# Hybrid decoder trunk on one core: key norms summed by a matrix of ones, five score products instead of six, rotary half turns by SBUF transfers

## The reference, cut to what matters

```python
q = (rms_norm(c_q, cq_g) @ w_uq).reshape(b_, t_, MLA_HEADS, QK_HEAD)      # 8 heads, 128 + 64 wide
ckv = rms_norm(c_kv, ckv_g)
k_nope = (ckv @ w_uk).reshape(...);  v = (ckv @ w_uv).reshape(...)
k = jnp.concatenate([k_nope, k_r], axis=-1)          # k_r: the 64 rotary key rows, the same for all heads
q = rms_norm(q, qn_g);  k = rms_norm(k, kn_g)        # over the 192 channels of a head
q, k = (rotary embedding on the last 64 channels)    # [x1 c - x2 s, x2 c + x1 s]
o = causal_block_attention(q, k, v)
```

## Time and profile before

| | |
|---|---|
| runs of the kernel | 1753.0, 1754.93, 1754.62 us; median 1754.62 us |
| profiled execution, its own time | 1751.97 us |
| its span | 1750.2 us |
| PE busy | 1734.3 us, 99% of the span, 12264 matmuls |
| DVE, ACT, POOL busy | 813.8, 467.3 and 1183.7 us |
| matmuls of `product`, share of the chain that ended last | 83% |
| one pair of heads (third pair of layer 0, from 348.8 to 446.3 us) | 97.5 us, of which PE is busy 97.4 |

### The profile page before, as it was taken

One profiled execution on the slowest core, in us unless ns is written; L12 is line 12 of the kernel. 1 busy time (PEld: TensorE's weight loads), 2 busy tenths in 40 slices (PEclk: granted clock), 3 DMA queues, 4 the chain that ended last, 5 costly groups with the idle time before them and its releaser, 6 DMA issues.

```text
span 1750.2 us, 32871 instructions
## 1 busy us (share of the span) xinstructions
PE 1734.3 (99%) x12264; PEld 1626.1 (93%) x12264; DVE 813.8 (46%) x1373; ACT 467.3 (27%) x843; POOL 1183.7 (68%) x1365
## 2 busy tenths in 40 slices
PE   7999999999999999999999999999999999999999
PEld 7999999999999999999999999989998888888887
DVE  7755546455555452212347546464555554422221
ACT  4423223242323331101134232332323233311110
POOL 7754746374798777777766647473847988777773
PEclk9999999999999999999999999999999999999999
DMA  4321212122322223222431312222222222422233
GB/s 158 123 96 54 90 59 84 65 74 70 109 84 84 84 96 130 88 96 85 161 112 64 105 56 74 72 84 68 72 77 104 85 93 86 145 88 92 96 121 110
DMA packets 47489, 161.60 MB, mean 92 GB/s; under 512 B 5408, under 2 KB 6816, under 8 KB 47136
## 3 DMA queue, kind: packets, MB, share of 16 engines
q1 hardware_dynamic: 41328, 146.56, 24.6%
q10 hardware_dynamic: 6112, 14.39, 2.2%
HBM read 152.27 MB, written 10.81 MB: 93 GB/s over the span
## 4 chain that ended last, share of the span: by engine, by line
PE 96%; DVE 2%; ACT 1%; issue 0%; ACTq 0%; DVEq 0%
PE slots L508 83%; PE slots L566 4%; PE slots L599 3%; PE slots L542 2%; PE slots L660 2%; PE slots L584 1%; PE slots L551 1%; DVE h_lo L1099 1%; DVE branch_lo L1111 1%; DVE h_tile L1175 0%; PE slots L701 0%; DVE spare L1120 0%; PE slots L569 0%; ACT cq_hi L849 0%; DVE early L1165 0%
## 5 line engine op out<-in xcount | busy, mean ns | idle before, releaser
L420 POOL TENSOR_TENSOR w_lo<-w_raw,w_hi 128x256 fp32r<-128x256 f32 x1004 | 828.4, 855 | 20.9
L415 POOL TENSOR_SCALAR w_hi<-w_raw 128x1024 fp32r<-128x1024 f32 x251 | 284.0, 1131 | 388.1 <-PE slots L508 380.7
L508 PE MATMUL slots<-h_hi,w_hi 128*128 128x264 f32 (+1 forms) x2112 | 522.8, 311 | 0.6
L508 PE MATMUL slots<-h_lo,w_hi 128*128 128x264 f32 (+1 forms) x2112 | 515.9, 308 | 0.0
L508 PE MATMUL slots<-h_hi,w_lo 128*128 128x264 f32 (+1 forms) x2112 | 515.1, 308 | 0.0
L508 PEld LDWEIGHTS slots<-h_hi,w_hi 128*128 128x128 f32 x2112 | 342.7, 188 | 22.9 <-issue 3.9
L508 PEld LDWEIGHTS slots<-h_hi,w_lo 128*128 128x128 f32 x2112 | 342.0, 188 | 19.1
L508 PEld LDWEIGHTS slots<-h_lo,w_hi 128*128 128x128 f32 x2112 | 342.0, 188 | 17.6
L508 PE MATMUL slots<-branch_hi,w_hi 128*128 128x264 f32 (+1 forms) x576 | 144.0, 313 | 9.6 <-DVE branch_lo L1111 8.9
L508 PE MATMUL slots<-branch_lo,w_hi 128*128 128x264 f32 (+1 forms) x576 | 142.8, 311 | 0.0
L508 PE MATMUL slots<-branch_hi,w_lo 128*128 128x264 f32 (+1 forms) x576 | 142.4, 311 | 0.0
(11 more groups left out here) (243 smaller groups left out, 2825.0 us busy)
## 6 DMA issues: line engine op xcount, KB each, us to landing
w_raw<-w_units SPq DMA_DIRECT2D x251, 512.0 KB, 3.2
stream<-sc_acc ACTq DMA_DIRECT2D x16, 264.0 KB, 3.0
sc_back<-stream SPq DMA_DIRECT2D x2, 2112.0 KB, 8.7
x_old<-stream SPq DMA_DIRECT2D x16, 264.0 KB, 4.4
stream<-residual_or_merged ACTq DMA_DIRECT2D x16, 264.0 KB, 2.5
ab_raw<-w_units SPq DMA_DIRECT2D x8, 512.0 KB, 4.6
residual_or_merged<-xt ACTq DMA_DIRECT2D x4, 528.0 KB, 7.6
stream<-xt ACTq DMA_DIRECT2D x1, 2112.0 KB, 10.3
```

Source lines behind the costliest of these rows:

```text
L415: pool.tensor_scalar(hi, raw, 1.0, 1.0, ALU.mult, ALU.mult).then_inc(sem("hi_part"), 1)
L420: op = pool.tensor_tensor(lo[:, cols], raw[:, cols], hi[:, cols].bitcast(F32), ALU.subtract)
L508: mm = pe.matmul(out[:, a_, 0:t1 - t0], w(k), x(k)[:, t0:t1], start=(n == 0), stop=(n == 3 * ks - 1))
```

## The change

1. The key norms no longer go by token sums and a diagonal. `spread_sum` multiplies a full matrix of ones with the squares themselves (two float32 products of 264 columns per head), so that each token's sum stands at once on all 128 partitions. It is issued right after `vb`. DVE adds the rotary part (`kr_sum`, made once per layer), ACT takes the root of the 128x528 tile, and DVE the reciprocal of the 128x528 tile, for each head. The ten sums `stat_k`, `spread_k0` and `spread_k1` and the ten diagonal pieces are gone.
2. The half turn is no product any more. ACT issues four transfers from SBUF to SBUF, of 32 rows each, as soon as DVE has written the rotary queries; the minus sign is in the sine table. The same once per layer for the rotary keys.
3. The rotary keys of a head are kept in both halves of the partitions (`kr_hi`, 128 rows), and `qr_both` holds for each head the high part of its rotary queries in 64 rows and the low part in the other 64. One product with `kr_hi` then gives hi x hi and lo x hi together: five products per score chunk instead of six.
4. The order in CQ is rearranged (`kr` before `q1`; the DVE work on `q1` later), and FILLS begins 5, 9 instead of 2, 12, with the sum of fills before the scores unchanged.

The core of the diff:

```diff
-FILLS = (2, 12, 5, 5, 6, 6, 7, 2, 6, 6, 7, 7, 6)
+FILLS = (5, 9, 5, 5, 6, 6, 7, 2, 6, 6, 7, 7, 6)
...
+            def spread_sum(out, squares):
+                for a_ in range(2):
+                    mm = pe.matmul(out[:, a_, 0:HALF], ones[0:squares.shape[0], :],
+                                   squares[:, a_ * HALF:(a_ + 1) * HALF], start=True, stop=True)
+                return mm
...
-                             (qn_lo[:, h, :], kn_hi[:, h, :]), (qr_hi, kr_hi[:, h, :]),
-                             (qr_hi, kr_lo[:, h, :]), (qr_lo, kr_hi[:, h, :])]
+                             (qn_lo[:, h, :], kn_hi[:, h, :]), (qr_both[:, h, :], kr_hi[:, h, :]),
+                             (qr_both[:, h, :], kr_lo[:, h, :])]
...
-                latent("kr", 4)
+                latent("q1", 4)
...
-                token_sums(out, [kr_sq[0:ROPE]]).then_inc(sem("cq_mm"), 1)
+                spread_sum(out, kr_sq[0:ROPE]).then_inc(sem("cq_mm"), 1)
...
+                    for h in range(2):
+                        out = free("ATT", l, p, f"sum_k{h}")
+                        pe.wait_ge(*at("k_squared", l, p, h + 1))
+                        spread_sum(out, ct[h]).then_inc(sem("att_mm"), 1)
...
-                            if c in stat_before:
-                                mm = token_sums(stat, ct[0:2], stat_before[c])
...
-                    for h in range(2):
-                        out = free("ATT", l, p, f"spread_k{h}")
-                        spread(out, ct[4 + h], lambda t: at("k_diag", l, p, h * NTOK + t + 1)).then_inc(sem("att_mm"), 1)
-                    out = free("ATT", l, p, "rot")
-                    pe.wait_ge(*was_read("ATT", l, p, "qr"))
-                    for a_ in range(2):
-                        mm = pe.matmul(out[:, a_, 0:HALF], rotate, ct[7][:, a_ * HALF:(a_ + 1) * HALF],
-                                       start=True, stop=True)
...
+            def turn_halves(dst, src, signal):
+                for first, second in ((0, 1), (1, 0)):
+                    for h in range(2):
+                        rows, other = (slice(ROPE * h + ROPE // 2 * n, ROPE * h + ROPE // 2 * (n + 1))
+                                       for n in (first, second))
+                        act.dma_start(dst[rows], src[other]).then_inc(sem(signal), 16)
...
-                    act.activation(k_ms[:], k_ms[:], ACT.Sqrt, bias=eps[0:TOK], scale=1.0 / QK).then_inc(
-                        sem("k_rms"), 1)
+                    for h in range(2):
+                        act.wait_ge(*was_read("ATT", l, p, f"sum_k{h}"))
+                        act.activation(ct[4 + h][:], ct[4 + h][:], ACT.Sqrt, bias=eps, scale=1.0 / QK).then_inc(
+                            sem("k_rms"), 1)
...
+                    act.wait_ge(*was_read("ATT", l, p, "qr"))
+                    turn_halves(spare[0][:], ct[7][:], "qr_turned")
...
+                        dve.tensor_tensor(halves(ct[4 + h][:]), slot(slot_of("ATT", f"sum_k{h}")), halves(kr_sum),
+                                          ALU.add).then_inc(freed("ATT", f"sum_k{h}"), 1)
+                    def k_inverse(h):
+                        dve.wait_ge(*at("k_rms", l, p, h + 1))
+                        dve.reciprocal(ct[4 + h][:], ct[4 + h][:]).then_inc(sem("k_rinv"), 1)
                     for g in range(2):
+                        k_inverse(g)
...
-                        dve.tensor_tensor(halves(ct[2 + h][:]), halves(ct[2 + h][:]), spread, ALU.mult).then_inc(
+                        dve.tensor_tensor(ct[2 + h][:], ct[2 + h][:], ct[4 + h][:], ALU.mult).then_inc(
                             sem("k_full"), 1)
-                        dve.tensor_tensor(halves(spare[1][rows]), halves(kr_full[rows]), spread[rows],
-                                          ALU.mult).then_inc(freed("ATT", f"spread_k{h}"), 1)
+                        dve.wait_ge(*at("k_full", l, p, h + 1))
+                        dve.tensor_tensor(ct[4 + h][:], kr_full, ct[4 + h][:], ALU.mult).then_inc(
+                            sem("kr_scaled"), 1)
...
-                    dve.tensor_tensor(halves(spare[0][:]), slot(slot_of("ATT", "rot")), halves(rope_sin),
-                                      ALU.mult).then_inc(
+                    dve.wait_ge(sem("qr_turned"), l * (64 * PAIRS) + p * 64 + 64)
                     dve.tensor_tensor(ct[7][:], ct[7][:], rope_cos, ALU.mult).then_inc(sem("qr_cos"), 1)
+                    dve.tensor_tensor(spare[0][:], spare[0][:], rope_sin, ALU.mult).then_inc(sem("qr_sin"), 1)
...
-                    lo_part(qr_lo[:], ct[7][:], qr_hi[:], "qr_lo")
+                    for h in range(2):
+                        rows = slice(ROPE * h, ROPE * h + ROPE)
+                        other = slice(ROPE * (1 - h), ROPE * (1 - h) + ROPE)
+                        dve.wait_ge(*at("qr_hi", l, p, h + 1))
+                        lo_part(qr_both[other, h, :], ct[7][rows], qr_both[rows, h, :], "qr_lo")
```

More of the change, by code:

```diff
@@ L566, in scores @@
                         mm = pe.matmul(bank[:, 0:k1 - k0], q[:, q0:q0 + nq], k[:, k0:k1], start=(m == 0),
-                                       stop=(m == 5 and not masked))
+                                       stop=(m == 4 and not masked))
                     if masked:
@@ L861, in _ @@
                     h_upper(k)
-                q_latent(1)
+                if l > 0:
+                    act.wait_ge(sem("stored"), l * (16 * KT))
+                act.wait_ge(*ready("CQ", l, 0, "kr"))
+                act.activation(halves(kr_gained[:]), slot(slot_of("CQ", "kr")), ACT.Identity, bias=zero,
+                               scale=hparam(l, KR_G)).then_inc(sem("kr_gained"), 1)
+                act.activation(halves(kr_sq), slot(slot_of("CQ", "kr")), ACT.Square).then_inc(freed("CQ", "kr"), 1)
                 act.wait_ge(*at("kv_ms", l, 0, 1))
@@ L880, in _ @@
                 q_latent(2)
+                act.wait_ge(*at("kr_normed", l, 0, 1))
+                turn_halves(spare[1][:], gatt[1], "kr_turned")
                 if l == 0:
@@ L1247, in _ @@
                     other = slice(ROPE * (1 - h), ROPE * (1 - h) + ROPE)
-                    for part in (kr_hi, kr_lo):
-                        dve.memset(part[other, h, :].bitcast(F32), 0.0).then_inc(sem("kr_blank"), 1)
+                    dve.memset(kr_lo[other, h, :].bitcast(F32), 0.0).then_inc(sem("kr_blank"), 1)
                 with dve.Fori(0, PAIRS) as p:
@@ L1324, in _ @@
                         dve.wait_ge(*at("krp_hi", l, p, h + 1))
-                        lo_part(kr_lo[rows, h, :], spare[1][rows], kr_hi[rows, h, :], "krp_lo")
-                    dve.wait_ge(*at("qr_hi", l, p, 1))
-                    lo_part(qr_lo[:], ct[7][:], qr_hi[:], "qr_lo")
+                        if h == 0:
+                            dve.wait_ge(*at("kr_blank", l, 0, 2))
+                        lo_part(kr_lo[rows, h, :], ct[4 + h][rows], kr_hi[rows, h, :], "krp_lo")
+                    for h in range(2):
+                        rows = slice(ROPE * h, ROPE * h + ROPE)
+                        other = slice(ROPE * (1 - h), ROPE * (1 - h) + ROPE)
+                        dve.wait_ge(*at("qr_hi", l, p, h + 1))
+                        lo_part(qr_both[other, h, :], ct[7][rows], qr_both[rows, h, :], "qr_lo")
                     dve.wait_ge(*at("q_rms", l, p, 1))
@@ L1602 @@
         kr = w_in[:, K_ROPE:K_ROPE + ROPE]
[L1603 to L1604 removed]
+        units += [cols(w_in, C_KV, n) for n in range(KV)] + [cols(w_in, C_Q, 0)]
+        units += [cols(np.concatenate([kr, kr], 1), 0, 0)] + [cols(w_in, C_Q, n) for n in range(1, KQ)]
         for p in range(PAIRS):
@@ L1645 @@
     x = np.concatenate([g["meta"], g["x"][0]], 0)
-    swap = np.zeros((P, P), np.float32)
-    half = ROPE // 2
-    for m in range(P):
-        first = m % ROPE < half
-        swap[m + half if first else m - half, m] = -1.0 if first else 1.0
     mask = np.where(np.arange(P)[None, :] > np.arange(P)[:, None], np.float32(MASKED), np.float32(0))
```

155 lines of the change are left out of this document (55 added, 100 removed), and 10 rows, old and new, of tables (SIGNALS, TILES).

## The result

The changed kernel takes 1775.57 us (median, 1772.99 to 1778.09), the kernel before beside it 1754.60; the ratio is 1.0121, 95% interval 1.0102 to 1.0140. Forecast were 1752, in the range 1728 to 1776, with 0.36 on slower. The time lies at the very end of the range, and it is slower where I had given the larger chance to faster. The two profiled executions lie further apart than the medians (1778.1 and 1752.0 us), so differences read from those two traces alone come out some 5 us larger.

What follows compares the result with a forecast made beforehand. PE, busy 99% of the span, was taken to bound the kernel. Per pair -0.1 + 1.4 - 1.56 = -0.26 us, eight pairs -2, CQ -1: 3 us less, say 1752 against the median 1754.62; range 1728 to 1776.

Steps and rivals of the forecast that it cites:

- PE's work: Ahead of each pair's scores: small sums and the exchange product go, so PE could begin the scores 3.4 us earlier.
- In the scores: Score chunks: one product of six goes, 1.56 us per pair, a clear gain of 12.5 us.
- The reciprocal: DVE's chain before the scores: each 128x528 reciprocal costs 3.2 us, by a straight line from small ones at 5.8 ns per element.
- I take the mean, 1.0: DVE's chain before the scores: seven products with both operands in SBUF at 1.0 us each, ends 0.76 and 1.2.
- The low parts: End of DVE's chain before the scores: 4.9 us for four becomes 7.1 us, the last being two at 1.1.
- 1.4 us each: Behind PE's 3.3 us wait at the scores: the clock falls in every pair, costing 1.4 us each; other end 0.
- Transfers: Half turn on ACT's queue: issues of 0.34 us, landing 3.0, 4.0 us in all, hidden behind four SBUF products on DVE.
- CQ: Once per layer: about 1.2 us less on PE, taken as 0.5 us gained per layer, ends 0 and 1.2.
- Rival D: Slower: two long reciprocals before the scores outweigh everything, 1762 to 1763; with SBUF products at 1.2 us, 1774; chance 0.28.

Runs made afterwards that it cites:

- The empty products: Changed kernel with ScalarE's copy of c0 moved earlier, plus 40 unread products per pair in front of PE's wait at the scores: 1755.9 us.
- the early copy: Changed kernel with ScalarE's copy of c0 moved ahead of its wait for the rotary queries: 1775.2 us, ratio 1.0116.

## Why the prediction was wrong

Right were the mechanism and its place: PE's saved work ahead of the scores turns into a wait for DVE's last low part, with half the clock behind it. Two terms of the sum were too small, and together they carry it over the line.

- **PE's work.** Forecast 3.4 us less ahead of the scores, the timeline has 3.2. In the scores 12.5 us in all were forecast; the run with this part alone shows 10, its pairs by themselves some 11.8 (8 x 1.48).
- **The reciprocal.** 3.2 us forecast from the slope of the small ones, 3.45 measured; (3448 - 164) / 527 is 6.2 ns per element, where I had 5.8. The Trainium skill ("VectorE: DVE Perf Modes", First, the fixed hardware budget) speaks of a repeat count of 8; read as eight cycles it gave an estimated 4.6 us, and the measurement decides against that reading. The two reciprocals added 0.5 us, but the sums and queries around them took less, so that the rotary queries were out of PSUM at 376.47 - 9.73 = 366.7, where I had 366.5.
- **The failed step, first: "I take the mean, 1.0"** for a product with both operands in SBUF. The seven run from 376.39 to 385.20, 8.8 us with their waits, where I had 7.25. By the run with GpSimd held back there are two prices, 0.71 and 1.24 or more, and no mean: all seven run while GpSimd works on SBUF, the first beside its sum of query squares, the others beside its splits. I had read the lock rule in the skill, wrote that by it all of them would cost the higher price, and didn't follow it. The low parts took 7.1 us as forecast. So the scores started at 392.68 - 9.73 = 382.95 in the times of before, 1.7 us after the forecast 381.25; before it was 381.34.
- **The failed step, second: "1.4 us each"** for the clock. I had one fall of 3.3 us in the trace and took it for every pair. The price of such a fall was about right (1.5 us where 3.4 us were at half rate); its length was not: behind the new pause PE stays low for 6.8 us in six pairs of eight. The empty products put the price at 2.4 us per pair, 8 us more in all.
- **Transfers.** An issue took 0.61 us (2.47 for the four on ScalarE's queue, timeline of the same pair), not 0.34, and landing 2.0 us, not 3.0. The two misses nearly cancel, 3 x 0.61 + 2.0 = 3.8 us against the forecast 4.0, and DVE doesn't wait for them here, since the four products ahead of the wait take 4.9 us. With those at 0.7 they are not hidden: in the run with GpSimd held back DVE waits 0.76 us per pair for them.
- **CQ.** Forecast 0.5 us less per layer. In the profile of the changed kernel the first values start 1.9 us later than before, but in that of the early copy, with the same CQ, 0.5 us earlier. The term is too small to be told from what differs between executions.

The sum by measured terms: 34.4 of wait and 19.3 of clock, less 25.9 (8 x 3.24 ahead of the scores) and 10.2 in the scores, is 17.6 us (16.0 with the 11.8 of the pairs); 21.0 were measured. The 3 to 5 us between them stay open. A likely place, not shown, is the half rate outside the pauses, 14.9 us in the changed kernel's profile and 4.7 in the one before. Against the forecast, 8 x 1.7 = 14 us lie in the start of the scores and 8 in the clock, together 22 of the 24 that were missed.

Rival D had the sign and, with its add-on of products at 1.2, even the number, 1774; but it named the reciprocals as the mechanism and made the products an afterthought. My own sum said that 0.1 us in a product is 5.6 us of time, and the row that I averaged reached from 0.76 to 1.18: the sign hung on a term that I had left at its mean, and slower deserved more than I gave it.

## What to carry to other kernels

When a change moves work from the busy engine to a chain that ends at the same point, what counts is how much of the busy engine's other work stands in front of that point: the order (here the fills) has to be set anew with it, and that alone was 43 us. Price an operation by its neighbours on the other engines, not by its group's mean; look for two prices in the trace and ask which partner runs beside each. And a pause of TensorE costs more than its length: put useful work in it, or count what the lower clock takes behind it.

## What the runs showed of the hardware beyond that

- The same SBUF product beside GpSimd's splits and without: 1.24 and 0.71 us, on 128x528 float32; the low parts of the keys 1.11 and 0.70.
- Pauses of the same length (2.65 to 2.69 us) at the same place were followed by 3.4 us at half rate in some pairs and by 6.8 us in others of one execution, two and six of the eight in the changed kernel. What decides between them no run here separates.
- 39 us of useless products (8 x 40 x 0.122) made a kernel 19.3 us faster.
- A transfer of 32 rows from SBUF to SBUF (66 KB) held ScalarE's queue 0.61 us for its issue, one of 128 rows to HBM 0.34 us.
